# The first steps of an adaLN transformer block with routed experts: the modulation's first quarter taken by eighths, and weight loads held back behind two gathers

## What is computed

```python
mod = silu(c) @ w_ada + b_ada                    # 6 x 1024; two parts are used at the start
sh_m, sc_m, g_m, sh_f, sc_f, g_f = split(mod, 6)
h = rmsnorm(x, norm_mix_g) * (1 + sc_m) + sh_m
z = h @ w_in                                     # u, v, pool and gates, 5120 columns
...                                              # spatial gating, pooling, two branches, w_out
hf = rmsnorm(x, norm_ffn_g) * (1 + sc_f) + sh_f
# router: each token picks 2 of 16 experts inside its best group
y = sum over experts of combine * ((silu(hf @ w_gate) * (hf @ w_up)) @ w_down)
out = rmsnorm(x + g_f * y, final_norm_g)
```

## Time and profile before

| | us |
|---|---|
| median of three runs | 761.75 |
| lowest and highest of them | 761.73, 763.98 |
| the profiled execution, its own time | 763.88 |
| its span in the trace | 761.5 |

### The profile page before, as it was taken

The page is one execution under the profiler, slowest core; times in us unless marked ns, Lnnn a source line. Parts: engine busy times, 40 slices in busy tenths (PEclk is TensorE's granted clock), DMA queues, the critical chain, the costliest instruction groups (busy, mean ns, idle before and its releaser), DMA issues.

```text
span 761.5 us, 10492 instructions
## 1 busy us (share of the span) xinstructions
PE 738.6 (97%) x3447; PEld 606.9 (80%) x3447; DVE 584.9 (77%) x709; ACT 392.0 (51%) x360; POOL 149.2 (20%) x121
## 2 busy tenths in 40 slices
PE   7999999999999999999999899999999999999995
PEld 6888888776888888887789677888888888888884
DVE  5884326764675766748768889999999999999985
ACT  5536333424222141323435267777777777777744
POOL 1000004102000000000054272523322323222313
PEclk9999999999999999999999999999999999999999
DMA  8989414211375472927372728799999999999992
GB/s 304 337 290 372 141 56 145 75 57 57 110 248 169 161 250 88 337 72 275 139 246 113 282 73 308 287 398 410 358 358 395 366 375 386 378 396 390 343 182 110
DMA packets 108996, 187.30 MB, mean 246 GB/s; under 512 B 7367, under 2 KB 58631, under 8 KB 108972
## 3 DMA queue, kind: packets, MB, share of 16 engines
q1 hardware_dynamic: 101420, 173.63, 62.9%
q0 software_dynamic: 5936, 11.71, 5.5%
q10 hardware_dynamic: 1616, 1.65, 0.7%
HBM read 180.00 MB, written 15.79 MB: 257 GB/s over the span
## 4 chain that ended last, share of the span: by engine, by line
PE 82%; DVE 9%; DMA 4%; issue 2%; ACT 1%; SPq 1%; POOL 0%; DVEq 0%; POOLq 0%; ACTq 0%
PE ps L1581 25%; PE ps L1583 25%; PE ps L1582 24%; DVE wsplit L893 2%; PE ps L1839 2%; PE ps L1931 1%; PE ps L1711 1%; DMA raw<-in_w_ada 1%; DVE raw L982 1%; DMA raw<-in_w_in 1%; PE ps L1772 1%; DMA raw<-in_w_out 1%; DVE raw L936 1%; PE ps L1875 1%; DMA work<-hf_rows,tok_idx 1%
## 5 line engine op out<-in xcount | busy, mean ns | idle before, releaser
L893 DVE TENSOR_TENSOR wsplit<-raw,wsplit 128x2048 fp32r<-128x2048 f32 x128 | 291.0, 2287 | 67.7 <-ACT wsplit L615 34.6
L802 ACT ACTIVATE wsplit<-raw 128x2048 fp32r<-128x2048 f32 x96 | 183.6, 1919 | 62.4 <-PE ps L1583 62.4
L1581 PE MATMUL ps<-wsplit,hgT 128*128 128x512 f32 x264 | 104.4, 395 | 1.1 <-DVE hgT L1363 1.1
L1583 PE MATMUL ps<-wsplit,hgT 128*128 128x512 f32 x264 | 103.0, 390 | 0.0
L1582 PE MATMUL ps<-wsplit,hgT 128*128 128x512 f32 x264 | 102.8, 389 | 0.0
L1581 PE MATMUL ps<-hT,wsplit 128*128 128x512 f32 x256 | 101.1, 395 | 1.1 <-DVE mx L1078 1.0
L1582 PE MATMUL ps<-hT,wsplit 128*128 128x512 f32 x256 | 99.6, 389 | 0.0
L1583 PE MATMUL ps<-hT,wsplit 128*128 128x512 f32 x256 | 99.6, 389 | 0.0
L936 DVE SCALAR_TENSOR_TENSOR raw<-raw,c_silu 128x256 f32 (+1 forms) x128 | 62.0, 485 | 13.7 <-DMA raw<-in_w_ada 9.7
L1581 PEld LDWEIGHTS ps<-wsplit,hgT 128*128 128x128 f32 x264 | 49.6, 188 | 11.1 <-issue 1.3
L1583 PEld LDWEIGHTS ps<-wsplit,hgT 128*128 128x128 f32 x264 | 49.5, 188 | 10.7
(11 more groups left out here) (310 smaller groups left out, 1214.0 us busy)
## 6 DMA issues: line engine op xcount, KB each, us to landing
raw<-in_w_exp_gate SPq DMA_DIRECT2D x32, 1024.0 KB
raw<-in_w_exp_up SPq DMA_DIRECT2D x32, 1024.0 KB
raw<-in_w_exp_down SPq DMA_DIRECT2D x32, 1024.0 KB
raw<-in_w_in SPq DMA_DIRECT2D x20, 1024.0 KB
raw<-in_w_ada SPq DMA_DIRECT2D x16, 1024.0 KB
raw<-in_w_ada SPq DMA_DIRECT2D x16, 512.0 KB, 5.6
expert_rows<-tmp SPq DMA_DIRECT2D x4, 1024.0 KB, 9.7
raw<-in_w_branch_a SPq DMA_DIRECT2D x4, 1024.0 KB
```

Of the source, the lines that this page charges most:

```text
L802: A_(wsplit[:, c, 0, :], raw[:, c, :], ACT.Copy).then_inc(hi_ready, 1)
L893: V.tensor_tensor(wsplit[:, n, 1, :], raw[:, slot, :], wsplit[:, n, 0, :].bitcast(F32), ALU.subtract).then_inc(lo_ready, 1)
L1581: nc.tensor.matmul(out, w_hi, m_hi_, start=first, stop=False)
L1583: return nc.tensor.matmul(out, w_lo, m_hi_, start=False, stop=last)
```

## The change

Two places change.

At the start, all four x tiles are loaded first. The first quarter of the modulation is loaded and computed by eighths (one feature block each; rows of 128 floats in place of 256), with shift and scale landing apart. Most sums over its rows are now products of PE with one column (`first_columns`, raw blocks times silu(c)); DVE sums four rows of the first block's scale and all eight of the second's shift (`block_sums`), and PE closes them with `summed_column`. The first value chunk comes in two halves, whose hi is made by ACT (`first_v_hi`) and no longer by DVE. DVE scales the fourth x tile too. The fourth tile is turned in parts between the modulation's products, the banks are saved one group after another (four saves before the second block), and the order of the first value groups follows.

At the experts' start, SP loads the second half of expert 0's `w_down` only when the first gather has landed, and the first `w_up` chunk of expert 1 (with all behind it) only when the second has. DVE takes `indices(1)` and the rows' lo before the lo of chunk M0 + 3, and `rows_lo(1)` before `select(2)` and the next weight lo. PE does 7 unread products in place of 16 ahead of the first gather.

```diff
-V_FIRST = ((0, 1), (1, 1), (2, 1), (2, 0), (3, 0), (0, 0), (1, 0))
+V_FIRST = ((0, 0), (0, 1), (1, 1), (2, 1), (2, 0), (3, 0), (1, 0))
...
+            def load_eighth(e):
+
+                chunk = raw[:, ADA_PLACE[e], :].rearrange("p (k s n) -> p k s n", k=ND, s=2)
+                for part, landing in ((0, ada_in[e]), (1, scale_in[e])):
+                    sp.dma_start(chunk[:, :, part, :],
+                                 shift_scale[:, :, part, e * P:(e + 1) * P]).then_inc(landing, 16)
+
+            def load_first_v(k, landing):
+
+                sp.dma_start(raw[:, V_PLACE[0], k * D:(k + 1) * D], w_in[:, k, D:2 * D]).then_inc(landing, 16)
...
-            load_x(0)
-            load_x(1)
-            load_ada(0)
-            load_x(2)
-            load_x(3)
-            load_ada(1)
-            load_v(0)
+            for t in range(NT):
+                load_x(t)
+            load_eighth(0)
+            load_first_v(0, value_in)
+            load_eighth(1)
+            load_first_v(1, landed[V_PLACE[0]])
             load_ada(2)
             sp.wait_ge(ada_used, 1)
...
-            for c in range(2):
-                load(c + 4, w_down[0, :, 2 * c:2 * c + 2, :], 2)
+            load(4, w_down[0, :, 0:2, :], 2)
+            sp.wait_ge(gathered, 16)
+            load(5, w_down[0, :, 2:4, :], 2)
+            sp.wait_ge(gathered, 32)
...
+            def x_saved(b, e):
+                A_(xT_kept[:, b:e, :], ps[:, b:e, :], ACT.Copy).then_inc(xT_saved, 1)
+
+            def x_block(k):
+                return ps[:, k, :] if k < 1 else xT_kept[:, k, :]
+
+            def h_block(k):
+
+                if k >= 1:
+                    act.wait_ge(xT_saved, 4)
+                A_(x_block(k), x_block(k), ACT.Identity, scale=gain[:, k:k + 1],
+                   bias=mod_cols[:, k:k + 1]).then_inc(h_aff, 1)
+                act.wait_ge(h_aff, k + 1)
+                A_(hT[:, 0, k, :], x_block(k), ACT.Copy).then_inc(h_hi, 1)
+
+            def first_v_hi(k):
+
+                c = slice(k * D, k * D + D)
+                return A_(wsplit[:, V_SPLIT[0], 0, c], raw[:, V_PLACE[0], c], ACT.Copy)
+
+            act.wait_ge(value_in, 16)
+            first_v_hi(0).then_inc(value_hi, 1)
             act.wait_ge(xT_t, NT)
-            def x_saved(b):
-                A_(xT_kept[:, b:b + 2, :], ps[:, b:b + 2, :], ACT.Copy).then_inc(xT_saved, 1)
-
-            x_saved(6)
-            x_saved(4)
-
-            def x_block(k):
-                return ps[:, k, :] if k < 2 else xT_kept[:, k, :]
-
-            def h_quarter(q):
-
-                act.wait_ge(gain_ready, q + 1)
-                for k in (2 * q, 2 * q + 1):
-                    if k >= 2:
-                        act.wait_ge(xT_saved, 3)
-                    A_(x_block(k), x_block(k), ACT.Identity, scale=gain[:, k:k + 1],
-                       bias=mod_cols[:, k:k + 1]).then_inc(h_aff, 1)
-                    act.wait_ge(h_aff, k + 1)
-                    A_(hT[:, 0, k, :], x_block(k), ACT.Copy).then_inc(h_hi, 1)
-
-            for q in range(4):
-                h_quarter(q)
-                if q == 0:
-                    x_saved(2)
-                if q < 3:
-                    hi(split_slot(q + 1), *raw_place(q + 1))
+            act.wait_ge(gain_ready, 1)
+            h_block(0)
+            act.wait_ge(xT_t, NT + 1)
+            x_saved(4, 6)
+            act.wait_ge(xT_t, NT + 2)
+            x_saved(6, 8)
+            x_saved(2, 4)
+            act.wait_ge(xT_t, NT + 3)
+            x_saved(1, 2)
+            act.wait_ge(landed[V_PLACE[0]], 16)
+            first_v_hi(1).then_inc(hi_ready, 1)
+            act.wait_ge(gain_ready, 2)
+            h_block(1)
+            for q in range(1, 4):
+                hi(split_slot(q), *raw_place(q))
+                act.wait_ge(gain_ready, q + 2)
+                h_block(2 * q)
+                h_block(2 * q + 1)
...
+            def block_sums(e, part, rows):
+
+                acc = macc_a[:, 0, e * P:(e + 1) * P]
+                for k in rows:
+                    w_k = raw[:, ADA_PLACE[e], (2 * k + part) * P:(2 * k + part + 1) * P]
+                    if k == rows[0]:
+                        ins = V.tensor_scalar(acc, w_k, c_silu[:, k:k + 1], None, ALU.mult)
+                    else:
+                        ins = V.scalar_tensor_tensor(out=acc, in0=w_k, scalar=c_silu[:, k:k + 1], in1=acc, op0=ALU.mult,
+                                                     op1=ALU.add)
+                    if k != rows[-1]:
+                        step(ins)
+                        done()
+                ins.then_inc(block_sum, 1)
+
+            def first_modulation(e):
+
+                dve.wait_ge(mod_mm, e + 1)
+                scale, shift_col = mod_cols[:, 8 + e:9 + e], mod_cols[:, e:e + 1]
+                step(V.tensor_tensor(scale, ps[:, MOD_BANK, 3 * P + 1:3 * P + 2], cols[:, 40 + e:41 + e], ALU.add))
+                V.tensor_tensor(shift_col, ps[:, MOD_BANK, 3 * P:3 * P + 1], cols[:, 32 + e:33 + e],
+                                ALU.add).then_inc(ada_used, 1)
+                done()
+                dve.wait_ge(ada_used, e + 1)
+                V.scalar_tensor_tensor(out=gain[:, e:e + 1], in0=scale, scalar=1.0, in1=cols[:, 8 + e:9 + e],
+                                       op0=ALU.add, op1=ALU.mult).then_inc(gain_ready, 1)
...
-            x_inverse(0)
-            x_inverse(1)
-            ada_head(0)
-            x_inverse(2)
-            x_inverse(3)
+            for t in range(NT):
+                x_inverse(t)
+            dve.wait_ge(scale_in[0], 16)
+            block_sums(0, 1, range(4, ND))
+            first_modulation(0)
+            dve.wait_ge(value_hi, 1)
+            v_lo(0, 0)
+            h_low(0)
             dve.wait_ge(consts, 2)
             step(V.reciprocal(inv_count[:, :], iota1[:, 0:16]))
-            ada_head(1)
-            dve.wait_ge(landed[raw_place(0)[0]], raw_place(0)[1])
-            step(v_hi(0))
-            modulation(0)
-            done()
-            v_lo(0, 0)
-            h_low(0)
-            v_hi(1).then_inc(hi_ready, 1)
+            dve.wait_ge(ada_in[1], 16)
+            block_sums(1, 0, range(ND))
+            dve.wait_ge(hi_ready, 1)
+            v_lo(0, 1)
+            first_modulation(1)
+            ada_head(2, range(2))
             h_low(1)
-            dve.wait_ge(h_lo, 2)
-            v_lo(0, 1)
             for q in range(1, 4):
-                ada_head(2 * q, range(4) if q == 1 else range(1, 4))
+                ada_head(2 * q, range(2 if q == 1 else 1, 4))
                 ada_head(2 * q + 1)
                 dve.wait_ge(hi_ready, q + 1)
                 v_lo(q, 0)
...
-            lo_n(M0 + 3, 3)
-            step(V.tensor_tensor(r_le, iota1[:, 0:TILES_MAX].unsqueeze(2).broadcast_to(ie),
-                                 r_cum.unsqueeze(1).broadcast_to(ie), ALU.is_gt))
-            done()
-            step(V.tensor_reduce(r_n, r_le, AX_X, ALU.add))
-            done()
-
             indices(1)
             for half in range(2):
                 dve.wait_ge((first_hi_half, hg_hi)[half], 1)
                 h_half = first_hi[:, 4 * half:4 * half + 4, :].rearrange("p k m -> p (k m)").bitcast(F32)
                 V.tensor_tensor(first_lo[:, 4 * half:4 * half + 4, :].rearrange("p k m -> p (k m)"),
                                 ps[:, 2 + half, :], h_half, ALU.subtract).then_inc((first_lo_half, hg_lo)[half], 1)
+            lo_n(M0 + 3, 3)
+            step(V.tensor_tensor(r_le, iota1[:, 0:TILES_MAX].unsqueeze(2).broadcast_to(ie),
+                                 r_cum.unsqueeze(1).broadcast_to(ie), ALU.is_gt))
+            done()
+            step(V.tensor_reduce(r_n, r_le, AX_X, ALU.add))
+            done()
...
             dve.wait_ge(hi_ready, M0 + 5)
             lo(0, 0)
+            rows_lo(1)
             select(2, expert_ahead(0))
...
                 if not prev:
-                    rows_lo(i + 1)
                     indices(i + 2)
                 lo_c(2)
...
+            def first_columns(e, part, rows):
+
+                for k in rows:
+                    col = (2 * k + part) * P
+                    nc.tensor.matmul(ps[:, MOD_BANK, 3 * P + part:3 * P + part + 1], raw[:, ADA_PLACE[e], col:col + P],
+                                     c_silu[:, k:k + 1], start=(k == 0), stop=(k == ND - 1))
+
+            def summed_column(e, part, first):
+
+                pe.wait_ge(block_sum, e + 1)
+                nc.tensor.matmul(ps[:, MOD_BANK, 3 * P + part:3 * P + part + 1], macc_a[:, 0, e * P:(e + 1) * P],
+                                 ones[:, 0:1], start=first, stop=True).then_inc(mod_mm, 1)
+
+            def turn_x(t, k):
+                return nc.tensor.transpose(ps[:, k, t * P:(t + 1) * P], x_tiles[:, t, k * P:(k + 1) * P], ident[:, :])
+
             pe.wait_ge(cols_ready, 1)
-            for t in range(NT):
-                idle_products((12, 3, 16, 0)[t], 3, 3 * P)
-                if t < 3:
```

(57 more changed lines are left out.)

27 lines of the change are left out of this document (10 added, 17 removed).

## The result

The changed kernel took 768.13 us (median of 11 executions, 765.11 to 770.81 and one of 838.58, at a granted clock of 0.845, that the comparison leaves out), the kernel before 762.65 (11 executions, 761.63 to 764.2). The ratio is 1.0064, 95% interval 1.0047 to 1.0081: slower, by about 5 us. The forecast was 763.4, with a range up to 765.6; it stood on a median of 761.75 for the kernel before, and on 762.65 it would be 764.3. Its likeliest case, +1.6 us, lay inside the bound of what can be told, and it gave a chance of 0.29 to a time above 764.0; the measured time lies outside the range.

What follows compares the result with a forecast made beforehand. The prediction took PE to bound the kernel (82% of the chain of waits), other engines counting only where PE waits. Start −0.6 and experts +2.2 gave +1.6 on a median of 761.75, so 763.4 us, range 760.0 to 765.6.

Steps and rivals of the forecast that it cites:

- likeliest case: The forecast's own sum over start and experts: +1.6 us on the whole time, given a chance of 0.42.
- The first gather: Experts' start: the first indirect transfer meets an empty queue and is turned by PE at 433.1, 2.5 us sooner.
- the placement that waits out a lo: POOL at the experts: the third table placement, starting at 436.63 inside the lo of M0 + 3, is caught until 437.95 + 0.9.
- the second gather that does not follow the first: POOL at the experts: behind four placements, the second gather starts at 440.4 and lands at 444.9, as before.
- DVE's idle time ahead of the rows' lo: DVE at the experts: done at 443.8, it waits 3.3 us until 447.13 because the rows come at the old time.
- PE's exit: PE leaving its last wait before the steady loop, at 471.22 before; the second term was read there, forecast at 473.
- the slow turn: PE's turn of the second gather's rows at half clock, costing 0.9 us that DVE inherits; part of the clock rival.
- the first term: The start: −0.6 us, PE work gone from behind its wait for DVE; ends −2.2 and +1.0.
- 43.29's place: The start: DVE's end of chunk 5 of the modulation, where the first term's gain of about 0.6 us was read.
- the first modulation: The start: the first eighth's modulation is in PSUM at 16.9, with gain at 17.4.
- the second term: The experts: +2.2 us at PE's last wait before the steady loop, from DVE's new order; ends +0.7 and +3.0.
- The clock: Rival: PE's longer wait before the second gather drops its clock, costing up to 1.7 us; time 765.0, chance 0.20.

Runs made afterwards that it cites:

- second and third profile of the changed kernel: The changed kernel unaltered, profiled twice more after its first profile of 768.8 us; these executions took 766.35 and 765.66 us.
- Experts alone: The change's experts part (held weights, DVE's new order, 7 unread products) on the start of the kernel before; ratio to before 1.0046.
- nothing held back: The changed kernel without the held weights (loads ahead of both gathers as before, 16 unread products), DVE's new order kept; ratio to before 1.0066.
- the profile with 16 products: The changed kernel with 16 unread products on PE ahead of the second turn, to keep the clock up; ratio to before 1.0074.
- the lo behind the rows: The changed kernel with the lo of slot 0 put behind the rows' lo of tile 1 on DVE; ratio to before 1.0091.

## Why the prediction was wrong

**Right.** The first gather (432.74 for 433.1), the placement that waits out a lo, the second gather that does not follow the first, DVE's idle time ahead of the rows' lo, and that PE's exit shows the loss. The second and third profile of the changed kernel have the forecast's order of events: third placement caught, exit at 44.8 and 45.2 for 42.6 before, +2.2 and +2.6 where the term said +2.2. Experts alone gave 44.71, +2.1. That the size agrees is luck in part: 0.8 and 0.6 of it is the slow turn, which the forecast had put into a rival, and DVE's order with the late `w_up` made only 1.4 and 2.0.

**Wrong, the first term** (−0.6). It was +0.6 at 43.29's place and 0.0 at the first gather. The mis-sized step is the first modulation, 18.1 in place of 16.9: the third x tile's squares began at 10.55, not 9.0, since ACT still waited 1.61 us for it. And what the term left at 43.29 could not live to 428, because the chain runs through waits for weight transfers at 223 and 352; I had followed the step to PE's next wait but not past it.

**Wrong, the second term** (+2.2). This is the step that failed: "Second gather: 440.4, landed 444.9, as before". It let placement two "pass" at 435.33 beside a lo forecast for 435.65; the lo came at 435.27. And it took the gather's own freedom from the lo of slot 0 for granted, although show it free by 0.18 us. In the profiled execution both were caught. Worked out by its own marks: rows' lo at 450.94 instead of 447.13 is +3.8, of which 2.9 are the landing and 0.9 the slow turn; from there to PE's exit 25.75 us against 24.09, +1.7. With nothing held back that stretch took 25.20, so about 1.1 of it is the selection and a lo that now stand behind the rows, and 0.6 is left for the late `w_up` and the slow clock (one profile each). 3.8 + 1.7 = 5.5. `index(2)` did not wait for the selection here: with the second turn so late and slow, PE came to it at 454.1, behind the selection's end at 453.2.

**The clock** came, and its first price (0.9 on the turn) was sized rightly; the profile with 16 products suggests that it adds nothing at the end while `w_up` is held behind the same landing, which no run with the weights free and the clock low has tested. The Trainium skill, "SBUF — State Buffer" (Who interferes with whom), lets VectorE with two SBUF inputs shut out GpSimd instructions that read SBUF; the traces agree: every indirect transfer that started 0.07 us or more behind the start of such a lo ended 0.85 to 0.95 us behind the end of a lo.

**Left open:** what moves POOL and DVE by 0.1 us against each other from one execution to the next, why the lo behind the rows cost 1.0091, and why a row of three lo holds an instruction to its end in some cases and not in others.

## What to carry to other kernels

An engine pair that shuts one another out turns an order into a lottery when their starts lie within 0.2 us: look for the margin, not only for who is first, and try the instruction on the critical path in front of those that it doesn't need (here, on the kernel before: the gather ahead of the placements, 1.7 us off PE's exit and 0.1% off the time). On the changed kernel the same move made the worst executions worse, 774 us. Taking a harmless wait away moves everything behind it, and may move it into such a collision. When a gain is followed, follow it through every later wait to the end; when times of one kernel spread over 5 us, profile it more than once before its profile is explained.

## What the runs showed of the hardware

- A placement or gather on POOL takes 0.98 to 1.11 us when nothing holds it; one that starts inside DVE's lo of 128x2048 ends about 0.9 us behind that lo's end (435.34 + 3.09 against 437.55; 441.65 + 2.96 against 443.70), one that starts 0.03 us ahead of it takes 1.00. A shorter DVE instruction with two inputs in SBUF does the same on its scale: the placement at 438.73 took 1.33 and ended 0.86 behind the end of one of 0.56 us. DVE's `first_lo`, with one input in PSUM, held none: a gather that started 0.6 us into it took 1.00.
- Three lo that follow each other without a gap: whatever started 0.64 to 0.70 us behind the start of the first was held through all three (6.86 to 6.96 us, eight cases in four profiles); whatever started 1.24 us or more behind the start of the first or second was held to the end of that one only (1.16 to 1.96 us, nine cases in six profiles, 451.69 of the kernel before with the gather first among them).
- Loads beside a gather: 3.3 us from the end of its instruction to PE's turn with the queue empty, 5.7 with loads at 357 GB/s.
